# Second block's feed-forwards: x's two parts as one 512-column operand past the high weights

## The reference

```python
def rms_norm_2(x, g):
    y = xf * lax.rsqrt(jnp.mean(xf * xf, axis=-1, keepdims=True) + RMS_EPS)
    return y * g

def swiglu(h, w1, w3, w2):
    return (jax.nn.silu(h @ w1) * (h @ w3)) @ w2

x = x + 0.5 * swiglu(rms_norm_2(x, ffn1_norm), ffn1_w1, ffn1_w3, ffn1_w2)   # before the mixer
x = x + 0.5 * swiglu(rms_norm_2(x, ffn2_norm), ffn2_w1, ffn2_w3, ffn2_w2)   # after it
```

## Time and profile before

| | |
|---|---|
| time, median of 3 runs | 1129.97 us (1129.5 to 1130.15) |
| time of the profiled execution | 1129.57 us |
| its span | 1127.7 us |
| PE busy | 1116.1 us, 99% of the span |
| DVE busy | 768.8 us, 68% |
| ACT busy | 559.5 us, 50% |
| POOL busy | 183.4 us, 16% |
| granted TensorE clock, mean | 0.998 of full speed |

### The profile page before, as it was taken

One profiled execution on the slowest core, in us unless ns is written; L12 is line 12 of the kernel. 1 busy time (PEld: TensorE's weight loads), 2 busy tenths in 40 slices (PEclk: granted clock), 3 DMA queues, 4 the chain that ended last, 5 costly groups with the idle time before them and its releaser, 6 DMA issues.

```text
span 1127.7 us, 22169 instructions
## 1 busy us (share of the span) xinstructions
PE 1116.1 (99%) x9610; PEld 1058.4 (94%) x9610; DVE 768.8 (68%) x1033; ACT 559.5 (50%) x671; POOL 183.4 (16%) x127
## 2 busy tenths in 40 slices
PE   9999999999999999999999999999999999999997
PEld 9999999998999999899999999999998989999996
DVE  4988978757786776775555567974278675554554
ACT  6433344494754554674444448622245656343343
POOL 3888783000000000000000010113030010000000
PEclk9999999999999999999999999999999999999999
DMA  8586553355456555546456565433144354655551
GB/s 271 188 289 201 184 187 112 117 211 174 138 197 203 201 170 186 178 147 215 156 186 210 161 202 157 129 92 99 41 142 136 136 182 155 205 185 187 187 185 39
DMA packets 147150, 190.01 MB, mean 168 GB/s; under 512 B 7659, under 2 KB 132139, under 8 KB 146943
## 3 DMA queue, kind: packets, MB, share of 16 engines
q1 hardware_dynamic: 145743, 184.32, 50.2%
q0 software_dynamic: 1264, 4.55, 1.2%
q10 hardware_dynamic: 64, 0.02, 0.0%
HBM read 187.79 MB, written 2.65 MB: 169 GB/s over the span
## 4 chain that ended last, share of the span: by engine, by line
PE 94%; DVE 3%; ACT 2%; issue 1%; ACTq 0%; DVEq 0%
PE bank L2196 22%; PE bank L2197 21%; PE bank L2198 21%; PE bank L2348 6%; PE bank L2349 6%; PE bank L2350 6%; PE bank L588 2%; PE bank L657 1%; DVE w_lo L1766 1%; PE bank L2280 1%; PE bank L2276 1%; PE bank L2436 1%; PE bank L562 1%; PE bank L2450 1%; PE bank L475 0%
## 5 line engine op out<-in xcount | busy, mean ns | idle before, releaser
L2196 PE MATMUL bank<-X_hi,w_hi 128*128 128x256 f32 x1760 | 502.5, 286 | 0.6 <-DVE w_lo L1766 0.5
L2197 PE MATMUL bank<-X_lo,w_hi 128*128 128x256 f32 x1760 | 497.9, 283 | 0.0
L2198 PE MATMUL bank<-X_hi,w_lo 128*128 128x256 f32 x1760 | 497.9, 283 | 0.0
L1464 ACT ACTIVATE w_hi<-w_raw 128x2048 fp32r<-128x2048 f32 x170 | 324.0, 1909 | 149.6 <-PE bank L2198 112.4
L1766 DVE TENSOR_TENSOR w_lo<-w_raw,w_hi 128x2048 fp32r<-128x2048 f32 x144 | 332.4, 2311 | 42.4 <-ACT w_hi L1464 42.0
L2196 PEld LDWEIGHTS bank<-X_hi,w_hi 128*128 128x128 f32 x1760 | 337.3, 192 | 6.3 <-issue 2.6
L2197 PEld LDWEIGHTS bank<-X_lo,w_hi 128*128 128x128 f32 x1760 | 337.4, 192 | 1.2
L2198 PEld LDWEIGHTS bank<-X_hi,w_lo 128*128 128x128 f32 x1760 | 337.3, 192 | 0.0
L1893 DVE TENSOR_TENSOR arena<-bank,rstd 128x512 f32<-128x512 f32 x66 | 45.6, 691 | 184.3 <-PE bank L2198 179.5
L1373 POOL TENSOR_TENSOR w_lo<-w_raw,w_hi 128x2048 fp32r<-128x2048 f32 x23 | 106.8, 4650 | 33.0 <-ACT w_hi L1464 32.9
L2348 PE MATMUL bank<-w_hi,Y_hi 128*128 128x512 f32 x264 | 103.3, 391 | 1.2 <-DVE Y_lo L1921 1.2
(11 more groups left out here) (302 smaller groups left out, 1404.5 us busy)
## 6 DMA issues: line engine op xcount, KB each, us to landing
w_raw<-in_ffn_w_dram SPq DMA_DIRECT2D x66, 1024.0 KB, 5.4
w_raw<-in_w_in_dram SPq DMA_DIRECT2D x52, 1024.0 KB, 5.2
w_raw<-in_w_up_dram SPq DMA_DIRECT2D x22, 1024.0 KB, 5.1
w_raw<-in_w_down_dram SPq DMA_DIRECT2D x11, 1024.0 KB, 4.9
w_raw<-in_w_out_dram SPq DMA_DIRECT2D x8, 1024.0 KB, 5.1
w_raw<-in_conv_pw_w_dram SPq DMA_DIRECT2D x4, 1024.0 KB, 5.1
w_raw<-in_w_attn_out_dram SPq DMA_DIRECT2D x2, 1024.0 KB, 4.9
w_raw<-in_rwkv_proj_dram SPq DMA_DIRECT2D x2, 1024.0 KB, 4.9
```

Source lines behind the costliest of these rows:

```text
L1464: a.activation(w_hi[slot][:, :], raw[slot][:, :], ACT.Copy).then_inc(S["w_hi"], told.one("w_hi"))
L2196: pe.matmul(o, wh, xh, start=start, stop=False, skip_group_check=True)
L2197: pe.matmul(o, wh, xl, start=False, stop=False, skip_group_check=True)
L2198: return pe.matmul(o, wl, xh, start=False, stop=stop, skip_group_check=True)
```

## The change

In the feed-forwards k = 1 and 2, for the pairs 1 to 10 (pair 0 stays as it was):

- `X_hi` and `X_lo` become the two halves of one tensor `X_both`, [128, 2, 8, 256]. `by_columns_wide` streams both at once past a block of high weights: one matmul of 512 columns (two runs of 256, one from each half), into all 512 columns of a bank of its own for each half m. The low weights meet `X_hi` alone, 256 columns, added into columns 256 to 511 of that bank. For each slice k the order is: high weights m = 0, m = 1, then low weights m = 0, m = 1.
- A chunk now fills two banks, so gates always use banks 2 and 3 and vals banks 0 and 1; `body_wide` waits for the evacuation of the pair before, not of the one before that.
- Each bank holds two sums that are to be added. ACT copies columns 256 to 511 of both banks to SBUF (`low_t`, `low_sums`), and DVE's `evacuate` adds them to columns 0 to 255.
- `rstd` is no longer multiplied in by DVE there. POOL, in a new `feed(k)`, multiplies the gate by `rstd` before SiLU and SiLU's result by `rstd` after it (`scaled`).
- ACT's order: the copy of gate i+1 and the rounding of G(i+2) come before SiLU i+1; the copy of val i comes before the rounding of V(i+1).
- In the mixer, six semaphores are merged into three, among them `decay_in` and `rate_in`, which come from two matmuls in a row, into one.

```diff
-        bank = [ctx.enter_context(nc.psum_tensor(f"bank{b}", [P, 512], F32)) for b in range(8)]
+        side_banks = [ctx.enter_context(nc.psum_tensor(f"banks{b}", [P, 2, 512], F32)) for b in range(2)]
+        bank = [side_banks[b // 2][:, b % 2, :] for b in range(4)]
+        bank += [ctx.enter_context(nc.psum_tensor(f"bank{b}", [P, 512], F32)) for b in range(4, 8)]
...
-        X_hi, X_lo = sb("X_hi", [P, NT, T], F32R), sb("X_lo", [P, NT, T], F32R)
+        X_both = sb("X_both", [P, 2, NT, T], F32R)
+        X_hi, X_lo = X_both[:, 0, :, :], X_both[:, 1, :, :]
...
+        low_t = region(3072, 2, 2 * T)
...
@@ POOL: feed(1) ahead of low_of(LOW_BY_POOL[0]), feed(2) at the end of its program @@
+            def feed(k):
+                for i in range(1, FPAIRS):
+                    pool.wait_ge(S["gate_read"], FPAIRS * k + i + 1)
+                    gate = u_t[:, 0].rearrange("p (m t) -> p m t", m=2)
+                    g.tensor_tensor(gate, gate, over(rstd[:], 2), ALU.mult).then_inc(
+                        S["scaled"], told.one("scaled"))
+                    pool.wait_ge(S["act_gate"], FPAIRS * k + i + 1)
+                    gate = act_t.rearrange("p (m t) -> p m t", m=2)
+                    g.tensor_tensor(gate, gate, over(rstd[:], 2), ALU.mult).then_inc(
+                        S["scaled"], told.one("scaled"))
...
@@ ACT, feed(k) @@
                 def gate_part(i):
-                    act.wait_ge(S["gate_read"], before + i + 1)
+                    if k == 0 or i == 0:
+                        act.wait_ge(S["gate_read"], before + i + 1)
+                    else:
+                        act.wait_ge(S["scaled"], scaled_count(k, 0, i))
...
+                def low_sums(side, i):
+                    if k == 0:
+                        return
+                    act.wait_ge(S["chunk_used"], b0 + 3 * i + side)
+                    a.activation(low_t[:, side].rearrange("p (m t) -> p m t", m=2),
+                                 side_banks[1 - side][:, :, T:2 * T], ACT.Copy).then_inc(
+                        S["low_copied"], told.one("low_copied"))
...
                 for i in range(1, FPAIRS - 1):
+                    low_sums(1, i)
                     val_part(i)
                     split(b0 + 3 * i + 3)
                     f_part(i)
                     split(b0 + 3 * i + 4)
+                    low_sums(0, i + 1)
+                    if k > 0:
+                        split(b0 + 3 * i + 5)
                     gate_part(i + 1)
-                    split(b0 + 3 * i + 5)
+                    if k == 0:
+                        split(b0 + 3 * i + 5)
+                low_sums(1, FPAIRS - 1)
...
@@ DVE, feed(k), evacuate(side, i, name) @@
-                    dve.wait_ge(S["rstd"], state["rstd"])
-                    v.tensor_tensor(u_t[:, side].rearrange("p (m t) -> p m t", m=2), pairs(2 * (i % 2) + side),
-                                    over(rstd[:], 2), ALU.mult).then_inc(S[name], told.one(name))
+                    o = u_t[:, side].rearrange("p (m t) -> p m t", m=2)
+                    if k == 0 or i == 0:
+                        dve.wait_ge(S["rstd"], state["rstd"])
+                        v.tensor_tensor(o, pairs(2 * (i % 2) + side), over(rstd[:], 2), ALU.mult).then_inc(
+                            S[name], told.one(name))
+                    else:
+                        dve.wait_ge(S["low_copied"], low_count(k, side, i))
+                        v.tensor_tensor(o, side_banks[1 - side][:, :, 0:T],
+                                        low_t[:, side].rearrange("p (m t) -> p m t", m=2), ALU.add).then_inc(
+                            S[name], told.one(name))
...
@@ DVE, feed(k), product(i) @@
-                    dve.wait_ge(S["act_gate"], before + i + 1)
+                    if k > 0 and i > 0:
+                        dve.wait_ge(S["scaled"], scaled_count(k, 1, i))
+                    else:
+                        dve.wait_ge(S["act_gate"], before + i + 1)
...
@@ PE @@
+            def by_columns_wide(n, slot, side):
+                split_ready(n)
+                for k in range(NT):
+                    for m in range(2):
+                        c = k * 256 + m * P
+                        pe.matmul(side_banks[1 - side][:, m, :].rearrange("p (a t) -> p a t", a=2),
+                                  w_hi[slot][:, c:c + P], X_both[:, :, k, :], start=k == 0, stop=False,
+                                  skip_group_check=True)
+                    for m in range(2):
+                        c = k * 256 + m * P
+                        mm = pe.matmul(side_banks[1 - side][:, m, T:2 * T], w_lo[slot][:, c:c + P], X_hi[:, k, :],
+                                       start=False, stop=k == NT - 1, skip_group_check=True)
+                mm.then_inc(S["chunk_used"], told.one("chunk_used"))
...
+                def body_wide(i, at, parity, first=False):
+                    if first:
+                        pe.wait_ge(S["rstd"], state["rstd"])
+                    else:
+                        pe.wait_ge(S["gate_read"], i + (before + 1))
+                    by_columns_wide(at + 2, (b0 + 2) % RING, 0)
+                    if first:
+                        pe.wait_ge(S["gate_read"], before + 1)
+                    pe.wait_ge(S["val_read"], i + (before + 1))
+                    by_columns_wide(at + 3, b0 % RING, 1)
+                    pe.wait_ge(S["f_lo"], i + (before + 1))
+                    rows_to_tokens(at + 4, (b0 + 1) % RING, (Y_hi, Y_lo), 2 * parity, first)
```

More of the change, by code:

```diff
@@ L321, in block_pair, with low_count, scaled_count @@
         act_t, f_t = region(2048, 2 * T), region(2560, 2 * T)
+        low_t = region(3072, 2, 2 * T)
+        def low_count(k, side, i):
+            return 2 * (FPAIRS - 1) * (k - 1) + 2 * (i - 1) + side + 1
+        def scaled_count(k, second, i):
+            return 2 * (FPAIRS - 1) * (k - 1) + 2 * (i - 1) + second + 1
         token_gain = region(8192, D)
@@ L514, in pe_mixer @@
             for t in range(HT):
-                decay = pe.matmul(bank[6 + t // 2][:, t % 2 * T:t % 2 * T + T], lora_w[96:P, 0, t * P:(t + 1) * P],
-                                  lora_act[96:P, 0, :], start=True, stop=True)
+                pe.matmul(bank[6 + t // 2][:, t % 2 * T:t % 2 * T + T], lora_w[96:P, 0, t * P:(t + 1) * P],
+                          lora_act[96:P, 0, :], start=True, stop=True)
                 rate_mm = pe.matmul(bank[4 + t // 2][:, t % 2 * T:t % 2 * T + T], lora_w[0:32, 1, t * P:(t + 1) * P],
                                     lora_act[0:32, 1, :], start=True, stop=True)
-            decay.then_inc(S["decay_in"], told.one("decay_in"))
-            rate_mm.then_inc(S["rate_in"], told.one("rate_in"))
+            rate_mm.then_inc(S["low_rank_up"], told.one("low_rank_up"))
             columns(B0 + 3)
@@ L803, in act_mixer @@
             split(B0 + 4)
-            for ready, b, dst, gain, done in (("decay_in", 6, dec, "rwkv_w0_2", "decay_read"),
-                                              ("rate_in", 4, rate, "rwkv_a0_2", "rate_read")):
-                act.wait_ge(S[ready], 1)
+            act.wait_ge(S["low_rank_up"], 1)
+            for b, dst, gain, done in ((6, dec, "rwkv_w0_2", "decay_read"), (4, rate, "rwkv_a0_2", "rate_read")):
                 for t in range(HT):
@@ L823, in act_mixer @@
                     S["g_read"], told.one("g_read"))
-            act.wait_ge(S["forget_abs"], 1)
+            act.wait_ge(S["low_rank_in"], 2)
             z = lora_in[32:32 + NH, 0, 1:T + 1]
@@ L828, in act_mixer @@
             a.activation(z, z, ACT.Ln, bias=ones[32:32 + NH, 0:1], scale=1.0).then_inc(
-                S["forget_log"], told.one("forget_log"))
+                S["decays"], told.one("decays"))
             a.activation(small[:, 62:63], ones[:, 0:1], ACT.Sqrt)
@@ L969, in dve_mixer @@
                                    scalar=col("mu_rate", 0, 0, 32), in1=lora_in[0:32, 1, 1:T + 1],
-                                   op0=ALU.mult, op1=ALU.add).then_inc(S["lora_shifted"], told.one("lora_shifted"))
-            dve.wait_ge(S["lora_shifted"], told.value("lora_shifted"))
+                                   op0=ALU.mult, op1=ALU.add).then_inc(S["low_rank_in"], told.one("low_rank_in"))
+            dve.wait_ge(S["low_rank_in"], told.value("low_rank_in"))
             split(B0 + 3)
@@ L980, in dve_mixer @@
             dve.wait_ge(S["dve_step"], told.value("dve_step"))
-            v.tensor_tensor(nabs, nabs, z, ALU.min).then_inc(S["forget_abs"], told.one("forget_abs"))
-            dve.wait_ge(S["forget_abs"], told.value("forget_abs"))
+            v.tensor_tensor(nabs, nabs, z, ALU.min).then_inc(S["low_rank_in"], told.one("low_rank_in"))
+            dve.wait_ge(S["low_rank_in"], told.value("low_rank_in"))
             shifted_columns(B0 + 1)
@@ L1039, in dve_mixer @@
             out_bank(B_FOX, fq[:, 0:2, :])
-            dve.wait_ge(S["decays"], 3)
+            dve.wait_ge(S["decays"], 4)
```

(25 more changed lines are left out.)

4 lines of the change are left out of this document (2 added, 2 removed).

## The result

The changed kernel takes 1122.14 us (median of 6 runs, 1121.55 to 1122.54) against 1130.06 for the kernel before in the same sessions: ratio 0.9932, 95% interval 0.9922 to 0.9942. That is 7.9 us less; the forecast was 1122.5, and 7.7 us less on PE.

A forecast was written before the change was run, and what follows sets the result against it. PE was taken to bound the kernel: 1129.57 - 7.7 (PE) + 0.2 (feed-forward edges) = 1122.1 us by the profiled execution, 1122.5 on the median. The range was 1119 to 1129 us.

The forecast's parts named there:

- What bounds the kernel: Whole span: PE busy 99%, the others 68% or less; what PE saves is saved if nothing takes its place.
- The price of the width: Changed chunks: 228 + 120 = 348 ns in place of 3 x 120 = 360; 40 chunks x 0.192 = 7.7 us.
- the two runs and the change of bank: Wide matmuls: both taken as 0, at worst the full 12 ns and no gain; as a rival, chance 0.18.
- Alternating widths at no cost: Within a chunk: long and short matmuls alternate, loading weights takes about 112 ns, under a short matmul's 120; no loss expected.
- DVE, ACT and POOL in a pass: Loop pass of 16.6 us: margins of 1.7 and 1.8 us before PE needs DVE's splits; nothing reaches PE.
- The ends of a feed-forward: At D10: Y_lo could slip past D10's start, up to 0.9 us twice; 0.2 taken in all.
- the slower rival: Loop: POOL and DVE hold each other up until PE waits 0.9 us a pass, 16 us, 1138.5 us; chance 0.08.
- The rival of better hidden loads: Changed chunks: 640 short matmuls lose 10 ns of pause each, another 6.4 us, 1116.1 us; chance 0.08.
- The skill's 2.5 ns a matmul: PE matmuls: columns over 2.4 GHz plus 2.5 ns; the merge would save 1.6 us, 1128.4 us, inside rival 1's span (1124.5 to 1130).

The follow-up runs named there:

- the mirrored order: The changed kernel with the two short matmuls of a slice swapped (high 0, high 1, low 1, low 0): 1121.97 us, ratio 0.9933.
- the first such order: The changed kernel with each slice ordered high 0, low 0, high 1, low 1: 1126.21 us, ratio 0.9968.
- the one across two banks: The changed kernel with slices 1 to 7 ordered high 0, low 1, high 1, low 0: 1125.10 us, ratio 0.9959.

## Why the prediction was right

- **What bounds the kernel.** PE alone, before and after; that whatever PE saves is saved was right, and undoing the width gave all of it back.
- **The price of the width.** 360 to 348 ns, 0.192 us a chunk, 3.84 us a feed-forward: measured 3.85 and 3.79. The sum was right, its two terms were not: the prediction named 228 ns for the wide matmul and called itself wrong at another value, and in the order of the change it is 233, made up by short ones of 115 in place of 120. That the two errors cancel was not foreseen, and in that part the number was luck: where the widths take turns one by one they do not cancel. A fixed pause for each instruction gives the right sum for a slice of this order, and not the price of each matmul. For the two runs and the change of bank the value 0 was taken from an interval; both are now shown to be 0, by one run of 512 and by the mirrored order.
- **Alternating widths at no cost** held for the order that the change has, which in fact keeps two of a width together, and not for all. The sentence gave a reason (a short matmul of 120 ns covers a load of 112) that holds for each order alike, and one order cost 4.1 us. That part of the reasoning was too short, though its number was right.
- **DVE, ACT and POOL in a pass.** The layout held to 0.1 or 0.2 us. Forecast from the start of val i: DVE's split ends at 3.55; POOL's gate product, released at 12.4, ends at 15.9, after waiting for the split; SiLU ends at 16.5. Measured in the changed kernel, POOL and then DVE and ACT in order of time:

```profile
521.66 3.27 POOL L1426 TENSOR_TENSOR arena<-arena,rstd 128x512 f32<-128x512 f32 x1 [11.28 <-DVE arena L1946]
525.67 1.29 POOL L1430 TENSOR_TENSOR arena<-arena,rstd 128x512 f32<-128x512 f32 x1 [0.74 <-ACT arena L1611]
```

```profile
521.50 2.28 DVE L1813 TENSOR_TENSOR w_lo<-w_raw,w_hi 128x2048 fp32r<-128x2048 f32 x1
526.46 0.69 DVE L1946 TENSOR_TENSOR arena<-banks,arena 128x512 f32<-128x512 f32 x1 [2.69 <-ACT arena L1633]
527.07 2.28 DVE L1813 TENSOR_TENSOR w_lo<-w_raw,w_hi 128x2048 fp32r<-128x2048 f32 x1
```

```profile
524.97 0.63 ACT L1611 ACTIVATE arena<-arena 128x512 f32<-128x512 f32 x1 [2.37 <-POOL arena L1426]
525.76 0.60 ACT L1633 ACTIVATE arena<-banks 128x512 f32<-128x512 f32 x1 [0.17 <-PE banks L2310]
```

  POOL stands until DVE's split ends at 523.78 and needs 1.2 us from there. That is the exclusion that the Trainium skill describes (SBUF — State Buffer, "Who interferes with whom"), again. ACT is done with SiLU 0.17 us before the val is ready, so POOL's delay ends just before it would begin to count; the split of G(i+1) is done at 529.35 and PE starts that chunk at 531.01, 1.66 us later (1.7 forecast).
- **The ends of a feed-forward.** 0 to 0.9 us each were allowed, 0.2 taken in all; 0 measured. POOL was served between the two splits:

```profile
654.35 3.27 POOL L1426 TENSOR_TENSOR arena<-arena,rstd 128x512 f32<-128x512 f32 x1 [11.28 <-DVE arena L1946]
658.37 2.56 POOL L1430 TENSOR_TENSOR arena<-arena,rstd 128x512 f32<-128x512 f32 x1 [0.74 <-ACT arena L1611]
```

```profile
654.19 5.58 DVE L1813 TENSOR_TENSOR w_lo<-w_raw,w_hi 128x2048 fp32r<-128x2048 f32 x2
...
662.49 0.69 DVE L1978 TENSOR_TENSOR Y_lo<-arena,Y_hi 128x512 fp32r<-128x512 f32 x1 [0.77 <-ACT Y_hi L1625]
```

  The second split then waited in turn (two take 5.58 us and not 4.5), and `Y_lo` ended at 663.18, 0.5 us before D10 started (663.71). In the kernel before it had been 2.0 us before (664.92 and 666.90). Of the two places that the prediction laid out, this is the narrower one, and not the 1.7 us in the loop on which it rested its case against the slower rival.
- **The slower rival** was real as a mechanism. In the loop it was out of reach by more than 1.3 us of POOL's time; at the end of a feed-forward it was not, since one more product there used up the 0.5 us and cost 3.4 us in all. Two cost 27; the prediction had priced the loop (16 us; 18.5 measured) and not what the end and the clock add. The rival of better hidden loads did not come about: short matmuls did start 115 ns apart, but the wide ones gave it back, and no order was faster than the changed kernel by more than 0.4 us.

The Trainium skill's line on access patterns (PSUM — Partial Sum Buffer, "Specifications (TRN2)") stands among the properties of PSUM. The operand in two runs lies in SBUF and is not what the line describes, and it cost nothing: 1121.94 us with one run, 1122.14 with two. The skill's 2.5 ns a matmul (TensorE: Matmul & The Clock Gate, "Back-to-back issue gap") is given there for an isolated matmul, without the loads of weights (the other section that the prediction names gives the time of a single matmul, not this gap). By it the gain would have been 1.6 us, an estimate; it was 7.6 by the stages and 7.9 by the medians, so the measured numbers decide.

## What to carry to other kernels

When a matmul costs its columns plus a fixed pause, and two matmuls in a row load the same weights, put their operands side by side and stream once: the gain is one pause each. Here two spacings of the old trace gave it to 0.1 us a feed-forward, though neither spacing held by itself afterwards. A loop with margin says nothing about its last pass: lay out the end of each loop too, because there the work that hid a chain is gone, and a wait of some us there can also cost the clock. Where short and long matmuls mix, keep two or more of a width together, and try the order on the chip. And where a helper engine gains nothing, leave it out: without POOL the time was the same here, and the last `Y_lo` was ready 0.8 us before D10 in place of 0.5.

## What the runs showed of the hardware that had not been expected

- Wide and short matmuls that take turns one by one need 353 ns a pair; in pairs, or 16 in a row, 347 to 348. In the first such order the down chunk behind was slower too, 5.50 us against 5.45 (the rest of its 0.20 us a pass); in the one across two banks it was not. The bank and the number of changes are excluded as causes; the cause is open.
- After 3.58 us and after 2.75 us of idle, TensorE's next matmuls of 512 columns started 0.43 us apart, the lower of its two clock levels (1.2 GHz), for over 3 us. After another idle of 2.8 us, in the first of the two feed-forwards of the run with two more POOL products, and after those of 1.2 to 1.4, they did not.
- Of two DVE instructions in a row with both inputs in SBUF, the second waits for a POOL product that had been waiting for the first: POOL gets its turn, and the two DVE instructions take 5.58 us in place of 4.5. This was seen at the end of both feed-forwards.
